# Starting the next projection before the last tiles of the norm are turned: both MLPs and layer 1 of a two-layer decoder trunk

## What is computed

```python
for layer in range(2):
    h = rms_norm(x, norm_mix_g[layer])
    z = h @ (even_w_in, odd_w_in)[layer]        # layer 1: 14 units of 128 columns
    mix = mixers(z) @ (even_w_out, odd_w_out)[layer]
    x = x + mix
    h = rms_norm(x, norm_mlp_g[layer])
    x = x + square(relu(h @ mlp_w_up[layer])) @ mlp_w_down[layer]   # 1024 -> 4096 -> 1024
```

## Time and profile before

| | |
|---|---|
| median of 3 runs | 2714.78 us (2711.61 to 2716.91) |
| the profiled execution | 2711.42 us, of which its span 2709.7 us |
| TensorE busy | 2499.4 us, 92% |
| VectorE, GpSimd, ScalarE busy | 1616.1, 1280.0, 1051.9 us |
| the three kinds of matmul of `products` (L2150 to L2152) | 22, 21 and 21% of the chain that ended last |
| mean granted clock of TensorE | 0.955 of full speed |

### The profile page before, as it was taken

The page is one execution under the profiler, slowest core; times in us unless marked ns, Lnnn a source line. Parts: engine busy times, 40 slices in busy tenths (PEclk is TensorE's granted clock), DMA queues, the critical chain, the costliest instruction groups (busy, mean ns, idle before and its releaser), DMA issues.

```text
span 2709.7 us, 31273 instructions
## 1 busy us (share of the span) xinstructions
PE 2499.4 (92%) x11133; PEld 1985.0 (73%) x11133; DVE 1616.1 (60%) x2354; ACT 1051.9 (39%) x1741; POOL 1280.0 (47%) x674
## 2 busy tenths in 40 slices
PE   6899798799778899999999989989988999999999
PEld 4677676355777688888888877766677888888887
DVE  6478568984886454445554755666444446544483
ACT  4255687556443433222232145435443222322220
POOL 4201233676763265556665712125515466655591
PEclk7999898799899899999999999988999999999999
DMA  4211123000300211112210222202002122111211
GB/s 148 51 28 28 32 67 91 15 8 13 117 16 1 63 55 39 34 58 62 62 46 24 70 98 55 63 16 74 24 19 60 47 62 62 54 37 33 62 62 62
DMA packets 164002, 136.57 MB, mean 50 GB/s; under 512 B 22969, under 2 KB 137730, under 8 KB 163906
## 3 DMA queue, kind: packets, MB, share of 16 engines
q1 hardware_dynamic: 152658, 124.58, 15.3%
q10 hardware_dynamic: 11248, 10.75, 1.5%
HBM read 116.17 MB, written 13.63 MB: 48 GB/s over the span
## 4 chain that ended last, share of the span: by engine, by line
PE 73%; DVE 10%; issue 8%; ACT 4%; POOL 2%; DMA 0%; ACTq 0%; DVEq 0%; POOLq 0%
PE ps L2150 22%; PE ps L2151 21%; PE ps L2152 21%; ACT signs L1218 1%; PE ps L2345 1%; PE ps L2504 1%; POOL cl L892 1%; PE ps L2262 1%; PE ps L2353 1%; DVE ub L2043 1%; DVE QL L1785 1%; PE ps L2333 1%; DVE ps L1723 1%; POOL w_lo L723 1%; DVE ps L1804 1%
## 5 line engine op out<-in xcount | busy, mean ns | idle before, releaser
L2150 PE MATMUL ps<-h_hi,w_hi 128*128 128x512 f32 x1680 | 670.8, 399 | 13.6 <-POOL w_lo L741 9.7
L2151 PE MATMUL ps<-h_lo,w_hi 128*128 128x512 f32 x1680 | 659.8, 393 | 0.0
L2152 PE MATMUL ps<-h_hi,w_lo 128*128 128x512 f32 x1680 | 659.4, 392 | 0.0
L2150 PEld LDWEIGHTS ps<-h_hi,w_hi 128*128 128x128 f32 x1680 | 319.4, 190 | 83.2 <-issue 14.4
L723 POOL TENSOR_TENSOR w_lo<-w_raw,w_hi 128x1024 fp32r<-128x1024 f32 x73 | 193.4, 2650 | 381.9 <-ACT w_hi L1228 376.9
L2151 PEld LDWEIGHTS ps<-h_lo,w_hi 128*128 128x128 f32 x1680 | 319.6, 190 | 67.8 <-issue 3.9
L2152 PEld LDWEIGHTS ps<-h_hi,w_lo 128*128 128x128 f32 x1680 | 318.9, 190 | 68.0
L2040 DVE TENSOR_TENSOR x_res<-ps,x_res 128x1024 f32<-128x1024 f32 x224 | 268.9, 1221 | 115.4 <-PE ps L2152 115.4
L2021 DVE TENSOR_TENSOR u_all<-ps,u_all 128x512 f32<-128x512 f32 x112 | 77.4, 691 | 416.0 <-ACT u_all L1125 416.0
L741 POOL TENSOR_TENSOR w_lo<-w_raw,w_hi 128x1024 fp32r<-128x1024 f32 x112 | 267.1, 2402 | 104.4 <-ACT w_hi L1114 104.4
L2150 PE MATMUL ps<-w_hi,uo_hi 128*128 128x512 f32 x784 | 307.5, 392 | 3.0 <-DVE shared L2040 3.0
(11 more groups left out here) (349 smaller groups left out, 4519.9 us busy)
## 6 DMA issues: line engine op xcount, KB each, us to landing
w_raw<-in_mlp_w_up SPq DMA_DIRECT2D x64, 512.0 KB, 4.0
w_raw<-in_mlp_w_down SPq DMA_DIRECT2D x64, 512.0 KB, 3.8
w_raw<-in_even_w_in SPq DMA_DIRECT2D x23, 512.0 KB, 3.7
x_res<-in_x SPq DMA_DIRECT2D x16, 512.0 KB, 8.8
w_raw<-in_odd_w_in SPq DMA_DIRECT2D x10, 512.0 KB, 3.6
scr_x<-x_res SPq DMA_DIRECT2D x8, 512.0 KB, 2.6
x_res<-scr_x SPq DMA_DIRECT2D x8, 512.0 KB, 4.3
out<-x_res SPq DMA_DIRECT2D x8, 512.0 KB, 2.6
```

The source lines that it names most:

```text
L2150: t_.matmul(out_, ah, bh, start=first, stop=False)
L2151: t_.matmul(out_, ah, bl, start=False, stop=False)
L2152: return t_.matmul(out_, al, bh, start=False, stop=last)
```

## The change

The first pass of each MLP's loop is written out ahead of the loop (`group(0, True)`, then the loop from 1), so that it can have waits of its own. In it, the projections of the first half of the tokens come first (all passes are mirrored for that), and the first one needs tiles 0 to 3 only. TensorE issues it ahead of the turns of tiles 6 and 7 (MLP 0), or between them (MLP 1); the second one waits for the last add. The weights of the first two units are loaded ahead of the last sum of the output projection. ScalarE rounds the first three among its steps of the norm, and GpSimd takes their lo parts; it zeroes `shared` between the second and the third. The output projection of layer 1 now sums into banks 0 to 3 and turns into 4 to 7, as layer 0's does, and waits for the banks of the attention ahead of its first turn.

For layer 1, unit 0's first half is projected ahead of the turns of tiles 6 and 7, then unit 1's first half, then the second halves of both. The places of units go round in the order 0, 3, 1, 2, so that unit 1's is free before MLP 0's last down projection. SyncE stores `x` behind unit 2's load and GpSimd zeroes `gw` behind unit 1's split. The turns of phase 2 use banks in a shifted order, so that the first projection's bank is the one of tile 4.

```diff
+        HALVES1 = [(0, 0), (1, 0), (0, 1), (1, 1)] + [(n, hf) for n in range(2, len(MIX1)) for hf in range(2)]
@@ slot_of
-                return (n - U_MIX1) % 4
+                return (0, 3, 1, 2)[(n - U_MIX1) % 4]
@@ unit_used
-                return proj_done, H_MIX1 + 2 * (n - U_MIX1) + 2
+                return proj_done, H_MIX1 + (n - U_MIX1 + 3 if n < U_MIX1 + 2 else 2 * (n - U_MIX1) + 2)
@@
-        S_UP = ((1, 1), (2, 1), (3, 1), (0, 1), (0, 0), (1, 0), (2, 0), (3, 0))
+        S_UP = ((1, 0), (2, 0), (3, 0), (0, 0), (0, 1), (1, 1), (2, 1), (3, 1))
@@ load_mlp, SyncE
-                sp.wait_ge(down_done, mlp_base(layer)[1])
-                with sp.Fori(0, S_ITERS) as i:
+                def group(i, begins=False):
                     for r, j in enumerate((1, 2, 3, 0)):
                         sp.wait_ge(w_ready, S_UNITS * i + (first + r - 3))
+                        if begins and r == 2:
+                            if layer:
+                                sp.wait_ge(att["st_done"], len(TILES[0]) + len(TILES[1]))
+                            else:
+                                sp.wait_ge(down_done, mlp_base(layer)[1])
...
+                group(0, True)
+                with sp.Fori(1, S_ITERS) as i:
+                    group(i)
@@ SyncE, layer 1's units
-                if n == 1:
+                if n == 2:
                     for t in range(T):
@@ split_mlp, GpSimd
-                pool.wait_ge(down_done, g0)
-                g.memset(shared[:], 0.0).then_inc(shared_zero, 1)
-                with pool.Fori(0, S_ITERS) as i:
+                def group(i, begins=False):
                     for r, j in enumerate((1, 2, 3, 0)):
                         low(i, r + 1, j, raws[r])
+                        if begins and r == 1:
+                            pool.wait_ge(down_done, g0)
+                            g.memset(shared[:], 0.0).then_inc(shared_zero, 1)
@@ GpSimd, layer 1's units
-                if n == U_MIX1:
+                if n == U_MIX1 + 1:
                     pool.wait_ge(n_turned, 48)
@@
-            return 0 if phase == 1 else 4
+            return 0 if phase % 2 else 4
         def turned_bank(phase, t, b):
+            if phase == 2:
+                return (2 * t + 2 + b) % 4 if t < 6 else 4 + (2 * t + b) % 4
             return 4 - first_bank(phase) + (2 * t + b) % 4
@@ ScalarE
+            def first_weights(layer, r):
+                _, g0, n0, _, _, _ = mlp_base(layer)
+                act.wait_ge(raw_landed[r], landed_mlp[n0][r] + 16)
+                act.wait_ge(down_done, g0 if layer else g0 - 16)
+                s.activation(w_hi[:, r + 1, :], raws[r], ACT.Copy).then_inc(w_hi_ready, 1)
@@ norm, ScalarE
                 for t in range(T):
+                    if phase == 3 and t == 7:
+                        first_weights(1, 0)
+                        first_weights(1, 1)
                     act.wait_ge(*x_ready(phase, t))
...
                     if t >= 1:
                         high(t - 1)
+                    if phase == 1 and 2 <= t < 4:
+                        first_weights(0, t - 2)
+                    if phase % 2 and t == 7:
+                        first_weights(phase // 2, 2)
                 high(T - 1)
@@ mlp, ScalarE
                     for r, j in enumerate((1, 2, 3, 0)):
+                        if begins and r < 3:
+                            continue
@@ ScalarE, layer 1: the loop runs over HALVES1
                 n = U_MIX1 + (p - H_MIX1) // 2 + 3
-                if n < U_OUT1:
+                if p % 2 == 0 and n < U_OUT1:
                     round_weights(n)
@@ conv, VectorE
-                dve.wait_ge(proj_free, H_MIX1 + 4 * j + 2)
+                dve.wait_ge(proj_free, H_MIX1 + (4 * j + 2 if j else 3))
@@ out_projection_of_attention, TensorE (of_recurrence: T in place of T + 2, too)
-                pe.wait_ge(x_added, g0)
-                pe.wait_ge(att["o_copied"], 4 * T)
-                for t in range(T + 2):
...
+                for t in range(T):
+                    pe.wait_ge(att["o_lo"], T + t + 1)
+                    down((h_hi, h_lo), list(range(4)), g0 + 2 * t, t, k0=4, bank0=first_bank(phase))
+                    if t == 2:
+                        pe.wait_ge(x_added, g0)
+                        pe.wait_ge(att["o_copied"], 4 * T)
+                        pe.wait_ge(att["o_norm"], 2 * T)
                     if t >= 2:
                         turn(phase, t - 2)
@@ mlp_by_halves, TensorE
+                def group(i, begins=False):
                     for p, (j, hf) in enumerate(S_UP):
+                        if begins:
+                            if p == 0 and layer:
+                                turn(phase, 6)
+                            if p in (0, 4):
+                                pe.wait_ge(n_lo, 16 * phase + (8 if p == 0 else 16))
+                            if p < 2:
+                                pe.wait_ge(x_added, g0 - 1 + p)
                         if p < 4:
                             pe.wait_ge(w_ready, S_UNITS * i + (n0 + p + 1))
                         pe.wait_ge(proj_free, 8 * i + (h0 + p - 3))
                         project(h0 + p, j, hf)
+                        if begins and p == 0:
+                            if not layer:
+                                turn(phase, 6)
+                            turn(phase, 7)
@@ TensorE, ahead of MLP 0 and MLP 1
-            pe.wait_ge(n_lo, 32)
-            pe.wait_ge(n_lo, 64)
@@ TensorE, layer 1
-            turn(2, T - 2)
-            turn(2, T - 1)
-            pe.wait_ge(n_lo, 48)
+            for n, hf in HALVES1:
+                kind, j, _ = MIX1[n]
+                if (n, hf) == (0, 0):
+                    pe.wait_ge(n_lo, 32 + 10)
+                elif n == 1 and hf == 0:
+                    turn(2, T - 2)
+                    turn(2, T - 1)
+                elif n == 0:
+                    pe.wait_ge(n_lo, 48)
+                project_unit_half(p, U_MIX1 + n, hf)
```

More of the change, by code:

```diff
@@ L779, in split_mlp @@
                     operand_low(i, 6, ub[:])
+                group(0, True)
+                with pool.Fori(1, S_ITERS) as i:
+                    group(i)
                 for n in range(n0 + S_UNITS * S_ITERS, n0 + MLP_UNITS):
@@ L1171, in mlp @@
                     operand(6, ub[:])
+                act.wait_ge(down_done, g0)
+                group(0, True)
+                with act.Fori(1, S_ITERS) as i:
+                    group(i)
                 h1, u1, q1 = h0 + 8 * S_ITERS, u0 + 7 * S_ITERS, q0 + 4 * S_ITERS
@@ new lines, in _ @@
+            for m, hf in HALVES1:
+                kind, j, _ = MIX1[m]
+                src = ps[:, p % 4, :]
+                if kind == "cg":
+                    act.wait_ge(proj_done, p + 1)
+                    if j >= 2:
+                        act.wait_ge(oc_ready, j - 1)
+                    s.activation(gel[:, j % 2, hf * HT:(hf + 1) * HT], src, ACT.Gelu_apprx_tanh).then_inc(proj_free, 1)
+                    if hf == 1 and j >= 1:
+                        root(j - 1)
+                elif kind == "cx":
+                    act.wait_ge(proj_done, p + 1)
+                    if j >= 2:
+                        act.wait_ge(conv_done, j - 1)
+                    s.activation(xpad[j % 2][:, 3 + hf * HT:3 + (hf + 1) * HT], src, ACT.Copy).then_inc(proj_free, 1)
+                    if hf == 1 and j >= 1:
+                        gates(j - 1)
+                elif kind == "dv":
+                    act.wait_ge(oc_ready, 4)
+                    values_part(nv, dv[:, 4 * hf:4 * hf + 4, :], p, vtmp1[:])
+                    nv += 1
+                else:
+                    if kind == "dq" and j == 0 and hf == 0:
+                        act.wait_ge(conv_done, 4)
+                    rope_part(1, kind, j, hf, p)
+                    if kind == "dq" and j == 0 and hf == 0:
+                        gates(3)
+                    if kind == "dq" and j == 1 and hf == 1:
+                        root(3)
+                    if kind == "dk":
+                        if hf == 0:
+                            query_root(1)
+                        key_root(1, hf)
+                p += 1
@@ L2044, in mlp_by_halves @@
                 dve.wait_ge(x_added, g0 + S_SUMS * S_ITERS)
-                for rows, fs in ((slice(0, 4), 1), (slice(4, 8), 0), (slice(4, 8), 1)):
+                for rows, fs in ((slice(4, 8), 1), (slice(0, 4), 0), (slice(0, 4), 1)):
                     dst = x[:, rows, fs * HT:(fs + 1) * HT]
@@ L2187, in out_projection_of_recurrence @@
                 pe.wait_ge(hg["att_read"], 8 * T)
[L2188 to L2192 removed]
+                for t in range(T):
+                    pe.wait_ge(hg["o_lo"], t + 1)
+                    down((h_hi, h_lo), list(range(4, 8)), g0 + 2 * t, t, n0 + 8 if t == 0 else None, k0=4,
+                         bank0=first_bank(phase))
                     if t == 2:
@@ L2232, in mlp_by_halves @@
                             ins.then_inc(down_done, 1)
+                group(0, True)
```

(29 more changed lines are left out.)

56 lines of the change are left out of this document (6 added, 50 removed).

## The result

The changed kernel takes **2689.51 us** as the median of four runs (2684.69 to 2694.09); the kernel before took 2715.85 on the same chip. The ratio is 0.9906, interval 0.9885 to 0.9927: faster by 26.3. The forecast was 2687.9 in a range of 2680 to 2697 and a gain of 26.9. The profiled execution took 2684.69, its span 2682.9, which is 26.8 less than the span before.

A forecast was written before the change was run, and what follows sets the result against it. TensorE was taken to idle at three places for the chain of norm and weights. Gains 8.3 + 10.5 + 8.1 = 26.9 take 2711.4 to 2684.5; against the median, 2687.9 us, range 2680 to 2697.

The forecast's parts named there:

- The three places: Ahead of MLP 0, layer 1's projections and MLP 1: second projection read earlier by 8.3, 10.5 and 8.1 us.
- MLP 0's start: Ahead of MLP 0: projection 0 starts at 922.25 instead of 932.17, behind tile 7's first add; gain there 8.3.
- The clock's price: First projection after a gap of TensorE: half clock makes its beginning slow, costing 1.5 us.
- 1.6 + 5.44: Ahead of MLP 0, after projection 0's read: two turns at 0.8 each, then projection 1 at 5.44.
- Layer 1: Ahead of layer 1's projections: projection 0 starts right behind turn 5, at 1602.8, and the clock stays; gain 10.5.
- The convolution's slack: Layer 1: the convolution ends at 1635.0, gate products are issued at 1638.2; slack 3.2, so no cost.
- Rival (c): Layer 1: ScalarE's hold behind unit 3 delays the convolution, gate products wait 5, total 2692.9; chance 6%.
- MLP 1: Ahead of MLP 1: projection 0 starts at 2032.5 instead of 2041.25, after turn 6; gain 8.1.
- read at start + 7.1: Ahead of MLP 1: projection 0, at the low clock, is read 7.1 us after its start at 2032.5.
- Beside the norm: GpSimd's two early splits beside VectorE's norm of tiles 2 to 4: at most 2.6 us, hidden, so no cost.
- The median: Whole kernel: profiled 2711.4 becomes 2684.5; runs' median lies 3.4 above the profile, giving a forecast of 2687.9.

The follow-up runs named there:

- the two halves of the change: The kernel before with only the layer 1 edits, 2703.89 us (ratio 0.9960); and with only the edits for both MLPs, 2701.58 us (ratio 0.9954).
- two other kernels: The kernel before with only the edits for both MLPs, 2701.58 us; the changed kernel with unit 2's cast moved behind tile 7's hi parts, 2686.39 us.
- the extra matmuls: The changed kernel with 16 unused matmuls in the gap ahead of each MLP's first projection; median 2685.10 us, ratio 0.9891.
- The two kernels with that gap: The changed kernel with tile 7's adds ahead of tile 5's lo parts, 2684.94 us; the same with MLP 1's first weight unit rounded earlier, 2678.02 us.
- the MLPs alone: The kernel before with all of the change's edits except those for layer 1; median 2701.58 us, ratio 0.9954.

## Why the prediction was right

- **The three places are the gain.** Shown by the stages and by the two halves of the change run alone: 25.0 of the 26.8 lie there.
- **MLP 0's start.** Forecast 5.30 after turn 5 (922.25), measured 5.33. The gate is the add of tile 7, shown by making it earlier. The clock's price was 1.5 forecast and 1.6 measured; that it fitted is in part luck, since behind the same start it was 2.8 in two other kernels (stages 21.05 and 21.10). The stage is 0.4 longer than forecast: the two turns and projection 1 take 7.43 (929.41 to 936.84), where I counted 1.6 + 5.44. Nearly all of it is in the 5.44, which is the distance of two reads back to back; projection 1 starts behind the turns at 931.07 and is read 5.77 later.
- **Layer 1.** Start forecast at 0.78 and measured 0.79 after turn 5 (1594.15 and 1594.94). The stage is 0.3 longer than forecast: turn 6 comes 0.13 later, and unit 1's first half is read 5.76 after its start (1603.31) in place of 5.6. The one gap is 0.92 and the clock stayed up. The convolution's slack was forecast as 3.2; it ends at 1628.15 and the gate products start at 1630.63, so it is 2.5. Rival (c) did not come true.
- **MLP 1: the step that was mis-sized** is "read at start + 7.1". The start was right, 6.47 forecast and 6.44 measured after turn 5. But projection 0 took 8.01 up to turn 7 (2012.62 to 2020.63), 0.9 more than ahead of MLP 0, as 12 of its matmuls ran slow. The price of the clock was 2.6 by the extra matmuls, and I had carried over the 1.5 of the earlier trace rows. The turn with what follows took 0.3 more than counted, again the 5.44 (2021.43 to 2027.16 is 5.73).
- **Beside the norm.** I allowed 2.6 for two splits that meet VectorE's `xn` and hid it. The two early splits (at 895.40 and 901.73) met none, and the `xn` of 904.81 stayed at 0.76. What I did not see is tile 7's `xn` ahead of MLP 1, in VectorE's and GpSimd's timelines:

```profile
2013.09 3.89 DVE L1516 TENSOR_SCALAR xn<-x_res,rstd 128x1024 f32<-128x1024 f32 x1
```

```profile
2010.01 4.68 POOL L754 TENSOR_TENSOR w_lo<-w_raw,w_hi 128x1024 fp32r<-128x1024 f32 x2 [50.77 <-ACT w_hi L970]
2014.63 1.80 POOL L765 MEMSET shared<- 128x2048 f32 x1
```

  It lost 3.1 and ended only when the clearing was over (2016.43). With the clearing behind the third split it met the two splits alone:

```profile
2010.74 2.15 DVE L1516 TENSOR_SCALAR xn<-x_res,rstd 128x1024 f32<-128x1024 f32 x1
```

  So 1.7 of the 3.1 came from the clearing and 1.4 from the splits. Projection 0 lay beside it, so it cost nothing there; without that cover I estimate that it would have cost all of it.
- **The median.** The forecast of 2687.9 is 1.6 below the first measurement of 2689.5 and 0.4 above the second of 2687.6. The terms were 1.9 too large in sum (26.9 against 25.0), and layer 1's attention, which no term of mine had, gave 1.8 back. That the median fits so closely is luck: two misses cancelled.

What stays open: what sets the moments at which the clock falls in layer 1's attention, so that the 1.8 came with the whole change and with neither half of it, and 2.3 more with the 16 extra matmuls at the MLPs (394.8 in place of 397.1), whose code in the attention is the same; and what decides whether it falls after a gap of 2.2. The two kernels with that gap differ only in edits ahead of MLP 1, over a thousand microseconds later, and one execution of each was profiled. That VectorE's wait for tile 5's hi parts is all that hid the other 0.6 of the clearing was read from one row and not tried by itself.

## What to carry to other kernels

Where an engine idles for a chain of norm and rounding, look for work of the next stage that needs only the tiles already done, and list all that gates it (inputs, weights, the bank it writes, what each queue has ahead); what is left of the idle time is then the latest of these, and moving two adds and a cast ahead and a clearing out of the way here brought another 10 on top of 26. Count a gap twice, once for its length and once for the slow matmuls behind it (half of the time that the engine then works at half the clock), and give the second a range, since it was 0 to 2.8 here. Compare traces by stages between fixed marks, when the span scatters by more than a term of the sum.

## What the runs showed of the chip that I had not expected

- The granted clock after a gap of TensorE, at the beginning of a projection, in the kernels with the new order: after 3.6 to 4.3 idle it was at 0.50 each time, and the slow stretch cost 1.6 to 2.8 (the stages of MLP 0 and MLP 1 less the 18.29 and 18.42 with the gaps filled); after 2.2 idle it fell once, 1.2 behind the restart, and stayed up once; after 0.9 to 1.5 it stayed up each time. The Trainium skill (TensorE: Matmul & The Clock Gate, Part 1: The HAM clock gate) calls the number of slow matmuls variable from run to run with the chip's free-running phase. The traces agree in that the number is not set by the gap: after like gaps ahead of MLP 0 it was 7 in the changed kernel and 13 in the one with the MLPs alone. That it varies from run to run of one kernel is not shown here: both profiles of the changed kernel have 7 ahead of MLP 0 and 12 ahead of MLP 1.
- A clearing of 128x2048 on GpSimd that reads nothing from memory made VectorE's `xn` 2.03 instead of 0.76, and splits followed by the clearing made it 3.89, where the splits alone made it 2.15.
